# Triangular inverse of a gated delta rule: its first four levels on 32x32 diagonal blocks in four array tiles

## What is computed

```python
m = jnp.where(strict, jnp.einsum('bhnid,bhnjd->bhnij', kb, k) * decay, 0.0)
a_mat = m + jnp.eye(C, dtype=m.dtype)
rhs = jnp.concatenate([v * beta[..., None], kb * jnp.exp(gc)[..., None]], axis=-1)
uw = lax.linalg.triangular_solve(a_mat, rhs, left_side=True, lower=True, unit_diagonal=True)
```

## Time and profile before

| | us |
|---|---|
| median of 3 runs | 1030.45 |
| lowest and highest of them | 1028.7, 1031.79 |
| the profiled execution, its own time | 1030.18 |
| its span in the trace | 1028.4 |

### The profile page before, as it was taken

How to read it: one execution, slowest core, us unless ns; L and a number is a source line. 1 busy time by engine, 2 the same in 40 slices (tenths; PEclk the granted TensorE clock), 3 DMA queues, 4 the chain that set the end, 5 groups by cost and what they waited for, 6 DMA issues and landing times. The chain is left out here.

```text
span 1028.4 us, 18086 instructions
## 1 busy us (share of the span) xinstructions
PE 994.6 (97%) x7583; PEld 888.6 (86%) x7583; DVE 676.1 (66%) x980; ACT 609.4 (59%) x945; POOL 119.2 (12%) x112
## 2 busy tenths in 40 slices
PE   6999999999999999999999999999999999999997
PEld 5999988878998888788886999888889979999985
DVE  5789675777775787886665655455459876454544
ACT  6779686736655667565666643434457975434342
POOL 1010055712001022530000200000001100000000
PEclk9999999999999999999999999999999999999999
DMA  9886255553677332255433665555553546556541
GB/s 336 316 248 181 91 171 197 171 171 101 219 257 245 128 126 80 83 181 188 153 113 104 187 216 171 200 170 203 171 157 124 181 147 205 194 175 200 169 163 41
DMA packets 116480, 178.25 MB, mean 173 GB/s; under 512 B 5204, under 2 KB 74098, under 8 KB 116400
## 3 DMA queue, kind: packets, MB, share of 16 engines
q1 hardware_dynamic: 115136, 174.01, 51.7%
q0 software_dynamic: 1120, 2.97, 0.9%
q10 hardware_dynamic: 144, 0.13, 0.0%
HBM read 176.05 MB, written 1.05 MB: 172 GB/s over the span
## 5 line engine op out<-in xcount | busy, mean ns | idle before, releaser
L1552 DVE TENSOR_TENSOR sb_w_lo<-sb_raw,sb_w_hi 128x2048 fp32r<-128x2048 f32 (+1 forms) x139 | 309.1, 2224 | 197.4 <-ACT sb_w_hi L815 197.2
L815 ACT ACTIVATE sb_w_hi<-sb_raw 128x2048 fp32r<-128x2048 f32 (+1 forms) x134 | 254.3, 1900 | 134.1 <-PE G L2447 109.4
L2445 PE MATMUL X<-sb_hT_hi,sb_w_hi 128*128 128x256 f32 x784 | 222.9, 284 | 1.4 <-DVE sb_w_lo L1552 0.8
L2446 PE MATMUL X<-sb_hT_lo,sb_w_hi 128*128 128x256 f32 x784 | 221.3, 282 | 0.0
L2447 PE MATMUL X<-sb_hT_hi,sb_w_lo 128*128 128x256 f32 x784 | 221.2, 282 | 0.0
L2445 PEld LDWEIGHTS X<-sb_hT_hi,sb_w_hi 128*128 128x128 f32 x784 | 149.4, 191 | 3.2 <-issue 0.9
L2446 PEld LDWEIGHTS X<-sb_hT_lo,sb_w_hi 128*128 128x128 f32 x784 | 149.4, 191 | 0.7
L2447 PEld LDWEIGHTS X<-sb_hT_hi,sb_w_lo 128*128 128x128 f32 x784 | 149.4, 191 | 0.0
L2445 PE MATMUL G<-sb_w_hi,sb_uT_hi 128*128 128x512 f32 x304 | 120.7, 397 | 0.9 <-DVE sb_uT_lo L2380 0.5
L2447 PE MATMUL G<-sb_w_hi,sb_uT_lo 128*128 128x512 f32 x304 | 120.1, 395 | 0.0
L2446 PE MATMUL G<-sb_w_lo,sb_uT_hi 128*128 128x512 f32 x304 | 120.0, 395 | 0.0
(11 more groups left out here) (534 smaller groups left out, 1869.0 us busy)
## 6 DMA issues: line engine op xcount, KB each, us to landing
sb_raw<-in_mlp_w SPq DMA_DIRECT2D x64, 1024.0 KB, 5.2
sb_raw<-in_ada_w SPq DMA_DIRECT2D x22, 1024.0 KB, 5.5
sb_raw<-in_b_in_w SPq DMA_DIRECT2D x16, 1024.0 KB, 5.5
sb_raw<-in_a_in_w SPq DMA_DIRECT2D x14, 1024.0 KB, 6.8
sb_raw<-in_sb_w_qkv SPq DMA_DIRECT2D x12, 1024.0 KB, 5.3
sb_raw<-in_rg_w_in SPq DMA_DIRECT2D x8, 1024.0 KB, 5.4
sb_raw<-in_a_out_w SPq DMA_DIRECT2D x4, 1024.0 KB, 5.0
sb_raw<-in_b_out_w SPq DMA_DIRECT2D x4, 1024.0 KB, 5.2
```

Source lines behind the costliest of these rows:

```text
L815: nc.scalar.activation(split_tile(w_hi, m)[:, 0:nk * w], raw_of(b)[:, 0:nk * w], ACT.Copy).then_inc(S["w_hi"], 1)
L1552: ins = nc.vector.tensor_tensor(split_tile(w_lo, m)[:, at], raw_of(b)[:, at], split_tile(w_hi, m)[:, at].bitcast(F32), ALU.subtract)
L2445: dt32(out, lh, rh, start=first, stop=False, skip_group_check=shared)
L2446: dt32(out, lh, rl, start=False, stop=False, skip_group_check=shared)
```

## The change

The first four levels (`l` = 0 to 3, blocks up to 32 rows) keep D, its turned copy and G as four diagonal 32x32 blocks a head: each at its own 32 partitions, 32 columns a head, 128 columns for four heads (`d32_of`, `d32T_of`, `g32_of`, `quarter_bank`). Each product or turn is four 32x32x32 matmuls a head, at four places on the diagonal of the array. Level 4 works on the 64x64 blocks as before. At level 3 the subtraction writes its result from the 32-wide layout into the 64-wide one, in four instructions of 32 partitions for each `m`; at level 1 DVE clears the 64-wide tile with two memsets.

```diff
+        def d32_of(m):
+            return diagonal(dd[m][:, :, :].rearrange("p h n -> p (h n)")[:, 4 * HALF:4 * (HALF + QUARTER)])
+        def d32T_of(m):
+            return diagonal(dd[m][:, :, :].rearrange("p h n -> p (h n)")[:, 4 * (HALF + QUARTER):8 * HALF])
+        def g32_of(m):
+            return diagonal(gs[m][:, :, :].rearrange("p h n -> p (h n)")[:, 0:4 * QUARTER])
+        QUARTERS = [slice(n, n + QUARTER) for n in range(0, P, QUARTER)]
...
# ACT, first turn and the copies of the turned D
-                    nc.scalar.activation(d_of(m), half_bank((X[0], TB[1])[m]), ACT.Copy).then_inc(S["d1"], 1)
+                    nc.scalar.activation(d32_of(m), quarter_bank((X[0], TB[1])[m]), ACT.Copy).then_inc(S["d1"], 1)
...
-                        if l < 5:
+                        if l < 4:
+                            nc.scalar.activation(d32T_of(m), quarter_bank((G[2], TB[1])[m]), ACT.Copy).then_inc(S["d1"], 1)
+                        elif l == 4:
...
# DVE
+                        if l < 4:
+                            lev = const("level")[:, l * QUARTER:(l + 1) * QUARTER].unsqueeze(1).to_broadcast([P, 4, QUARTER])
+                            nc.vector.tensor_tensor(g32_of(m), quarter_bank((G[0], G[3])[m]), lev, ALU.mult).then_inc(S["inv_gs"], 1)
...
+                    if l == 1:
+                        for m in range(MT):
+                            ch.mark(nc.vector.memset(d_of(m), 0.0))
...
+                        if l < 3:
+                            nc.vector.tensor_tensor(d32_of(m), d32_of(m), change, ALU.subtract).then_inc(S["inv_d"], 1)
+                        elif l == 3:
+                            ch.settle()
+                            for b in QUARTERS:
+                                ins = nc.vector.tensor_tensor(d_of(m)[b, :, b.start % HALF:b.start % HALF + QUARTER], d32_of(m)[b],
+                                                              change[b], ALU.subtract)
+                            ins.then_inc(S["inv_d"], 1)
...
# PE, the product M D (the turn and the second product change in the same way)
+                            if l < 4:
+                                for b in QUARTERS:
+                                    ins = dt32(quarter_bank((G[0], G[3])[m])[b, h, :], mt_[m][b, h, b], d32_of(m)[b, h, :],
+                                               start=True, stop=True)
+                            elif l == 4:
```

More of the change, by code:

```diff
@@ L58 @@
 HALF = 64
+QUARTER = 32
 CONST = {}
@@ L61 @@
 for _name, _n in (("ident", P), ("ones", P), ("eps", 1), ("tiny", 1), ("cum", P), ("neg_incl", P), ("neg_strict", P),
-                  ("level", 5 * HALF), ("level1T", P), ("suffix", P), ("neg_ones", P), ("blockmask", 8)):
+                  ("level", 4 * QUARTER + HALF), ("level1T", P), ("suffix", P), ("neg_ones", P), ("blockmask", 8)):
     CONST[_name] = (_at, _n)
@@ L95, in make_consts @@
     put("neg_strict", np.where(b > a, 0.0, NEG))
-    r, q = a % HALF, np.arange(HALF)[None, :]
-    levels = [((r // (2 * s) == q // (2 * s)) & (r % (2 * s) >= s) & (q % (2 * s) < s)) for s in (2, 4, 8, 16, 32)]
+    levels = []
+    for s in (2, 4, 8, 16, 32):
+        n = max(2 * s, QUARTER)
+        r, q = a % n, np.arange(n)[None, :]
+        levels.append((r // (2 * s) == q // (2 * s)) & (r % (2 * s) >= s) & (q % (2 * s) < s))
     put("level", np.concatenate(levels, axis=1))
@@ L612, in half_bank, with quarter_bank @@
             return diagonal(bank[:, 0:4 * HALF])
+        def d32_of(m):
[4 more added lines that the diff above has]
+            return diagonal(gs[m][:, :, :].rearrange("p h n -> p (h n)")[:, 0:4 * QUARTER])
+        def quarter_bank(bank):
+            return diagonal(bank[:, 0:4 * QUARTER])
         def corner_bank(m):
@@ L1844, in _ @@
                         product = half_bank((G[0], G[3])[m])
-                        if l < 5:
-                            lev = const("level")[:, l * HALF:(l + 1) * HALF].unsqueeze(1).to_broadcast([P, 4, HALF])
+                        if l < 4:
+                            lev = const("level")[:, l * QUARTER:(l + 1) * QUARTER].unsqueeze(1).to_broadcast([P, 4, QUARTER])
+                            nc.vector.tensor_tensor(g32_of(m), quarter_bank((G[0], G[3])[m]), lev, ALU.mult).then_inc(S["inv_gs"], 1)
+                        elif l == 4:
+                            lev = const("level")[:, 4 * QUARTER:].unsqueeze(1).to_broadcast([P, 4, HALF])
                             nc.vector.tensor_tensor(g_of(m), product, lev, ALU.mult).then_inc(S["inv_gs"], 1)
@@ L1868, in _ @@
                             dve.wait_ge(S["inv_d"], j - 1)
-                        if l < 5:
+                        change = quarter_bank((G[1], TB[0])[m])
+                        if l < 3:
[6 more added lines that the diff above has]
+                            ins.then_inc(S["inv_d"], 1)
+                        elif l == 4:
                             nc.vector.tensor_tensor(d_of(m), d_of(m), half_bank((G[1], TB[0])[m]), ALU.subtract)\
@@ L2786, in inverse_T @@
                     for h in range(4):
-                        for b in (UPPER, LOWER):
-                            ins = dt32(half_bank((X[0], TB[1])[m])[b, h, :], ddT[m][b, h, b], ident[b, b], start=True, stop=True)
+                        for b in QUARTERS:
+                            ins = dt32(quarter_bank((X[0], TB[1])[m])[b, h, :], ddT[m][b, h, b], ident[b, b], start=True, stop=True)
                     ins.then_inc(S["d1T"], 1)
@@ L2862, in _ @@
                         if l >= 1:
+                            turned_bank, d = (quarter_bank, d32_of(m)) if l < 4 else (half_bank, d_of(m))
                             for h in range(4):
-                                for b in (UPPER, LOWER):
-                                    ins = dt32(half_bank((G[2], TB[1])[m])[b, h, :], d_of(m)[b, h, :], ident[b, b],
+                                for b in QUARTERS if l < 4 else (UPPER, LOWER):
+                                    ins = dt32(turned_bank((G[2], TB[1])[m])[b, h, :], d[b, h, :], ident[b, b],
                                                start=True, stop=True)
@@ L2883, in _ @@
                         for h in range(4):
-                            if l < 5:
+                            if l < 4:
+                                for b in QUARTERS:
+                                    turned_d = ddT[m][b, h, b] if l == 0 else d32T_of(m)[b, h, :]
+                                    ins = dt32(quarter_bank((G[1], TB[0])[m])[b, h, :], turned_d, g32_of(m)[b, h, :],
+                                               start=True, stop=True)
+                            elif l == 4:
                                 for b in (UPPER, LOWER):
-                                    turned_d = ddT[m][b, h, b] if l == 0 else dT_of(m)[b, h, :]
-                                    ins = dt32(half_bank((G[1], TB[0])[m])[b, h, :], turned_d, g_of(m)[b, h, :],
+                                    ins = dt32(half_bank((G[1], TB[0])[m])[b, h, :], dT_of(m)[b, h, :], g_of(m)[b, h, :],
                                                start=True, stop=True)
```

## The result

| | before | after |
|---|---|---|
| median of 4 runs each, us | 1029.58 | 1042.45 |
| lowest and highest | 1028.4, 1031.79 | 1041.84, 1043.28 |
| the profiled execution, its own time | 1030.18 | 1042.23 |
| its span | 1028.4 | 1040.4 |

The change makes the kernel slower: ratio 1.013, 95% interval 1.0117 to 1.0143. The forecast was 1034.4 with a range up to 1040, so the direction was right and the size three times too small.

What follows compares the result with a forecast made beforehand. The prediction took PE's own instruction order to bound the kernel. Level terms of 2.2 and 1.25 us plus 0.8 for DVE's subtractions made 4.2 us on 1030.2, so 1034.4 us, range 1025.5 to 1040.

Steps and rivals of the forecast that it cites:

- What bounds the kernel: Whole span and both inverses: PE's own order bounds, PE busy 97% of the span, ACT close behind in the inverses.
- the price of a group: Levels 0 to 3: 64 PE records a group at 13 ns each, 0.83 us, 0.37 more than now.
- the sign of its own error: Level 2: the forecast is wrong if groups come closer than 0.47 us.
- its sign for being right: Groups about 0.83 us apart, level 2 of the first head group over 5 us, ACT idle longer before its copies.
- The level sums: Levels 0 to 3 at 13 ns a record: +2.2 us in the first head group, +1.25 in the second.
- DVE's eight subtractions: End of level 3, ahead of level 4: 1.1 us per `m` instead of 0.4, mostly hidden; +0.8 us over both head groups.
- Behind the inverses nothing gives time back: After the inverses: PE's 1.95 us wait for DVE's L1770 hangs on a DVE chain that moves with the second inverse.
- The faster rival: Levels 2 and 3: stream keeps up, four tiles run side by side, ACT takes over; 1027.3 or 1025.5 us; chance 0.33.
- The slow-pace rival: Levels 0 to 3: records as slow as today's groups, 14.6 ns or worse; 1039 us and above; chance 0.06.

Runs made afterwards that it cites:

- `shift`: The changed kernel with 64 tiny matmuls replacing four clock fillers near the start, 120 more PE instructions ahead of the untouched inverses; 1044.85 us, ratio 1.0141 against the kernel before.
- `sub1`: The changed kernel with only one of the four 32-partition subtractions at the end of level 3, three left out; 1041.5 us, ratio 1.0126 against the kernel before.
- `pairs`: The changed kernel with each four-tile matmul serving two heads with one weight (64 moving columns), halving the group's matmuls; 1028.56 us, ratio 1.0004 against the kernel before.

## Why the prediction was right in direction, half by luck, and wrong in size

- **What bounds the kernel** held: PE's own order does, and the loss came on PE.
- **The failed step is the price of a group.** It took 13 ns a record from L2587's stretch as the pace of the stream, and 0.83 us for a group. Groups come 0.27 us apart at full clock and 0.43 to 0.45 at half, which is 4.2 and 7 ns a record. L2587's pace was not the stream's. It was that of matmuls all in one tile, at a time when 256-column matmuls went at 0.21 us and not at 0.12, as the prediction itself noted; `shift`'s 64 tiny ones, in the same place of the array and of the run, have it as well, a matmul and a load every 27 ns. Which of the two sets it, no run separates. The text named as the sign of its own error "groups closer than 0.47 us", and that is what came. A stream was indeed too slow, but it has no steady price per instruction: it is free inside a block of 256 and stands at the border. Only the average over a block, 3.7 us or some 14.5 ns an instruction, is a pace; that this is also what two-tile groups hold today is chance. At 4.2 ns the prediction's own sum gives a gain. It was right to suspect the stream, but the direction came from a wait that its sum does not hold, and so did its sign for being right: level 2 of the first head group took 5.80 us, over 5, with groups 0.43 to 0.45 us apart.
- **The level sums** were 2.2 and 1.25 us; measured 6.7 and 8.9. Level 0 came out at +0.02 and -0.3 where +0.4 and 0 stood. The largest terms, +4.0 at level 1 and +3.7 at level 4 of the second head group, stood at nothing: no rate of PE's would put them there. They are one late packet each, with the half clock behind it. These are the terms that the sum put at nothing without a reason: I took DMA as having "no instruction more or less" and did not ask what DMA brings to PE itself (6 packets more); and the granted clock I had only looked at in the past, not as something that PE's stops would cost.
- **DVE's eight subtractions**: 0.4 in each head group foretold, 0.43 measured at each level 4. The row of before that priced them gave 1.1 us for four, and they take 1.18. `sub1` can't tell whether this reaches the end.
- **"Behind the inverses nothing gives time back"** was wrong by 3.1 us. The chain of DVE did move with the inverse, but it doesn't keep its length: without POOL beside it, it is 1.8 us shorter, and PE's wait for L1770 (now L1789) nearly vanished.
- **The faster rival** was right on the array: four tiles work side by side, and a group came under 0.3 us. Its limit was right too: it gave level 2 of the first head group 3.4 us when ACT is the bound, and `pairs` has 4.08 with a stop of 0.74 in it (136.27 to 140.35). What it missed is that DVE's masks come in beside ACT; at the end `pairs` shows no gain (ratio 1.0004) where 2.9 us less stood. The skill's rule named there, TensorE: Matmul & The Clock Gate, "Part 3: Packing small matmuls", agrees with these rows in that the tiles overlap, though it has starts 4 ns apart and here a matmul comes every 8.5 ns, each with a load. (That the trace of before agreed for two tiles was true of the overlap alone: there it was 29 ns.) Its "Back-to-back issue gap", 25 ns at least between starts, doesn't hold across tiles and would have led to 0.80 us a group, as wrong as my 0.83.
- **The slow-pace rival**, 1039 and above, has the number that came, with a chance of 0.06, but not the mechanism: it had groups at 14.6 ns a record or worse, and they came at 4.2 and 7. Its reason (no long stretch of float32 records is denser than today's) was an honest warning all the same: in the trace of before no two borders lie closer than 5.0 us, and I priced a jump beyond that by a local pace.

What stays open: how the loss splits between stops and low clock. The stops are 9.5 us of the 15.7 lost in the inverses; no run held the clock up while all the stops stayed. The stops themselves vary between runs with where the weight loads fall (12.3 us in the profiled run of `shift`, 12.2 in that of `sub1`), and their times much less (1043.8 and 1042.2 us, against 1042.2).

## What to carry to other kernels

Splitting work into more and smaller PE instructions has a price that no instruction's row shows: count matmul and load records over a few microseconds, and if 256 of them come in under about 3.7 us (5.5 with the DMA queues full), expect PE to stop at block borders, as here, and perhaps to lose its clock by it. The sign in a profile is a wait on "issue" in the middle of a uniform group, at a fixed distance in instructions. Before speeding up an engine's part of a balanced loop, look at who is next: here half the group time brought nothing, as PE's waits for ACT and DVE rose from 2.1 to 9 us.

## What was not expected of the hardware

- Behind a stop, the packet of the next block starts 1.1 us after the border, takes 1.1 us, and PE goes on 1.4 us later. It queues behind weight transfers that began before it: 2.9 us to its start at a DMA share of 0.90 and 0.99, and 4.3 at 0.99 in the second head group (border 201.41, packet 205.75). A high share alone doesn't do it: with a load near its end it was 1.2 us at a share of 1.08. A transfer load that the kernel before doesn't feel (ratio 1.0003 without it) goes with half of the change's loss.
- 32 matmuls and 32 loads in four tiles take 0.27 us, 8.5 ns a matmul, while a same-tile matmul with its load takes 59 ns with 64 columns.
- The place of a stop is set by PE's instruction count from the start of the program: 120 instructions more at 26 us moved stops at 130 to 210 us to other lines, and the ratio from 1.013 to 1.0141, within the intervals.
- DVE's 128x512 instruction of L1790 takes 1.64 us beside a busy POOL and 0.75 without it.
- A turn of the 32x32 blocks on DVE takes 0.42 us for 128x256 and replaces 32 PE instructions and a copy of ACT at no loss, where DVE has room.
